# Fifteen conditioning chunks as VectorE multiply-and-sum steps, and context tiles in the router's waits

## The reference, cut to what matters

```python
def ada_params(cond, w, b):             # cond 1024, w 1024 x 6144, b 6144
    m = jax.nn.silu(cond) @ w + b
    return jnp.split(m, 6, axis=-1)     # shift1, scale1, gate1, shift2, scale2, gate2

h = modulate(rms_norm(x, g), sh1, sc1)          # h * (1 + sc1) + sh1
p = h @ w_in + b_in                             # first block: 1024 -> 6656
...
h2 = modulate(rms_norm(x, g2), sh2, sc2)
x = x + gt2 * moe_ffn(h2)               # 32 experts in 4 groups, two per token
```

## Time and profile before

| | |
|---|---|
| Three runs | 1829.98, 1832.39, 1832.53 us; median 1832.39 |
| The profiled execution | span 1829.5 us from the first to the last instruction; a device time of its own is not given, so the shortest run, 0.5 us above the span, stands for it |
| TensorE busy | 1767.4 us, 97% of the span |
| VectorE busy | 462.7 us, 25% |
| ScalarE busy | 324.7 us, 18% |
| HBM read | 470.29 MB; 257 GB/s over the span |
| Mean granted TensorE clock | 0.996 of full speed |

### The profile page before, as it was taken

The page is one execution under the profiler, slowest core; times in us unless marked ns, Lnnn a source line. Parts: engine busy times, 40 slices in busy tenths (PEclk is TensorE's granted clock), DMA queues, the critical chain, the costliest instruction groups (busy, mean ns, idle before and its releaser), DMA issues. The chain is left out here.

```text
span 1829.5 us, 24606 instructions
## 1 busy us (share of the span) xinstructions
PE 1767.4 (97%) x10866; PEld 1344.7 (73%) x10866; DVE 462.7 (25%) x1010; ACT 324.7 (18%) x732; POOL 0.2 (0%) x4
## 2 busy tenths in 40 slices
PE   6999999999999999999999999999999999999997
PEld 4674887888664466676667577688888876888886
DVE  5310124525125221111101144531100135411001
ACT  4110013103214111010000123521100125211000
POOL 0000000000000000000000000000000000000000
PEclk9999999999999999999999999999999999999999
DMA  9453677467999999999999973365444331554430
GB/s 380 177 224 116 259 316 280 185 253 268 372 391 414 401 421 420 421 421 421 398 421 407 421 291 118 139 241 181 153 161 140 113 116 46 215 200 161 142 111 23
DMA packets 61810, 472.93 MB, mean 259 GB/s; under 512 B 7719, under 2 KB 11208, under 8 KB 12040
## 3 DMA queue, kind: packets, MB, share of 16 engines
q1 hardware_dynamic: 60472, 470.08, 65.7%
q10 hardware_dynamic: 1232, 1.28, 0.2%
HBM read 470.29 MB, written 1.05 MB: 258 GB/s over the span
## 5 line engine op out<-in xcount | busy, mean ns | idle before, releaser
L2520 PE MATMUL bank<-hT,ring 128*128 128x256 f32 x1024 | 221.5, 379 | 0.0
L2539 PE MATMUL bank<-second_work,ring 128*128 128x256 f32 x1024 | 221.3, 379 | 0.0
L2539 PEld LDWEIGHTS bank<-second_work,ring 128*128 128x128 f32 x1024 | 194.6, 190 | 26.5
L2520 PEld LDWEIGHTS bank<-hT,ring 128*128 128x128 f32 x1024 | 194.4, 190 | 26.4
L1345 PE MATMUL bank<-hT,ring 128*128 128x256 f32 x704 | 160.8, 385 | 4.5 <-issue 2.7
L1345 PEld LDWEIGHTS bank<-hT,ring 128*128 128x128 f32 x704 | 133.1, 192 | 39.8 <-issue 12.9
L650 PE MATMUL bank<-hT,ring 128*128 128x256 f32 x704 | 153.9, 379 | 0.0
L650 PEld LDWEIGHTS bank<-hT,ring 128*128 128x128 f32 x704 | 133.5, 191 | 18.8 <-issue 1.2
L1813 PE MATMUL bank<-ring,rowsT 128*32 128x512 f32 x1008 | 117.5, 597 | 1.2 <-DMA ring<-in_expert_w 1.0
L1345 PE MATMUL bank<-tmp,ring 128*128 128x256 f32 x384 | 86.5, 382 | 5.9 <-DMA ring<-in_w_out 4.3
L1345 PEld LDWEIGHTS bank<-tmp,ring 128*128 128x128 f32 x384 | 71.9, 190 | 24.8 <-DMA ring<-in_w_out 7.8
(11 more groups left out here) (468 smaller groups left out, 1707.5 us busy)
## 6 DMA issues: line engine op xcount, KB each, us to landing
ring<-in_expert_w SPq DMA_DIRECT2D x190, 1024.0 KB, 12.2
ring<-in_w_ff SPq DMA_DIRECT2D x96, 1024.0 KB, 7.1
ring<-in_ada_w SPq DMA_DIRECT2D x36, 2048.0 KB, 10.4
ring<-in_w_in SPq DMA_DIRECT2D x29, 1024.0 KB, 8.2
ring<-in_w_in SPq DMA_DIRECT2D x13, 2048.0 KB, 8.8
ring<-in_w_out SPq DMA_DIRECT2D x12, 1024.0 KB, 6.0
ring<-in_ret_w_o SPq DMA_DIRECT2D x2, 2048.0 KB, 8.2
ring<-in_w_out SPq DMA_DIRECT2D x2, 2048.0 KB, 12.8
```

The costliest lines, as they stand in the source:

```text
L2520: mm = pe.matmul(ff_bank(n), w[:, k, (n % 2) * P:(n % 2 + 1) * P], hT[:, k, xs], start=k == 0, stop=k == DT - 1)
L2539: mm = pe.matmul(ff_bank(FT + i), w[:, f, :], W[:, 16 * h + f, :], start=h == f == 0, stop=h == 1 and f == FT // 2 - 1)
```

## The change

The 12 chunks A0 to A11 and the three of the router stage are no longer multiplied on TensorE. The host stores their 15 weights transposed (`rows_first`), so that a 2 MB chunk R holds 4 x 128 output features, one per partition, with the 1024 inputs along it. The condition vectors (three of them) are loaded as rows that stand in all partitions, and ScalarE applies Silu to them. VectorE then does, for each 128 features and each condition needed, one `scalar_tensor_tensor` over 1024 columns with a sum (`accum_out`) into `mods`. R0 to R6 belong to `ada_w_2` and need both conditions, 8 steps each; R7 to R14 belong to `ada_w` and need one, 4 steps each: 88 steps.

All 15 stand in the input stage now. The order of the ring there is W0 W1 R0 W2 R1 W3 R2 R3 W4 R4 R5 W5 R6 W6 R7 W7 R8 R9 W8 R10 W9 R11 R12 W10 R13 R14 W11 W12. The steps of an R chunk are dealt evenly over the tiles of the W chunk that follows it: VectorE does them behind the emptying of each tile. An R chunk's slots are free when its last step is done. In the router stage TensorE does (-1, 0) first, (-1, 1) and (-1, 2) behind the token transposes, (-1, 3) behind the ranks and (0, 0) behind `gather(0)`.

```diff
+        ROW_CHUNKS = [(1, j) for j in range(4)] + [(0, j) for j in range(3)] + [(None, j) for j in range(8)]
...
         plan_both("in", [wide("w_in", j) for j in IN_CHUNKS],
-                  [wide("ada_w", j) for j in range(ADA0, 12)] + [wide("ada_w_2", j, 1) for j in range(4)],
-                  [0, 0, 1, 1, 1, 1, 1, 1, 2, 1, 1, 1, 1])
+                  [features_first(("ada_wT_2_0", "ada_wT_2_1", "ada_wT")[-1 if l is None else l], j) for l, j in ROW_CHUNKS],
+                  [0, 1, 1, 2, 2, 1, 1, 2, 1, 2, 2, 0, 0])
...
-        plan_both("ada2_router", [wide("ada_w_2", j, 0) for j in range(8, 12)], in2_views[0][0:2], [0, 0, 0, 2])
+        plan_both("ada2_router", [wide("ada_w_2", 8, 0)], in2_views[0][0:2], [2])
...
+                    row_steps = [(n, i, m) for n, job in enumerate(row_jobs) for i in range(4) for m in range(len(job[3]))]
...
+                        follows = min(t[0] for t in tiles if t[0] > job[0])
+                        tiles_of_next[n] = [i for i, t in enumerate(tiles) if t[0] == follows]
...
+                    def row_steps_after(i):
+                        here = [s for s, (n, _, _) in enumerate(row_steps) if i in tiles_of_next[n]]
+                        if not here:
+                            return range(0)
+                        where = tiles_of_next[row_steps[here[0]][0]]
+                        done = lambda t: here[0] + len(here) * t // len(where)
+                        return range(done(where.index(i)), done(where.index(i) + 1))
+
+                    def weigh(dve, s):
+                        n, i, m = row_steps[s]
+                        chunk, mod, first, conds = row_jobs[n]
+                        if i == m == 0:
+                            wait_chunk(dve, chunk)
+                        w = chunk_tile(chunk, D)[:, i, :]
+                        if len(conds) == 2 and s >= 2:
+                            dve.wait_ge(S("weighed"), s - 1)
+                        nc.vector.scalar_tensor_tensor(out=w if m == len(conds) - 1 else products_out, in0=w, scalar=1.0,
+                                                       in1=cond_rows[conds[m]], op0=ALU.mult, op1=ALU.mult,
+                                                       accum_out=mod[:, first + i, m:m + 1]).then_inc(S("weighed"), 1)
...
+                        for s, (n, i, m) in enumerate(row_steps):
+                            freed[row_jobs[n][0]] = (S("weighed"), s + 1)
...
-                                for n in due(i):
-                                    if n == 0:
-                                        pe.wait_ge(S("hy_spec_out"), 4)
-                                    beside.pe(pe, n)
... (SyncE, ahead of the early tables and of W1)
+                            for m in (0, 2, 3):
+                                sp.dma_start(cond_rows[m], a["cond_rows"][m:m + 1, :].to_broadcast([P, D]))\
+                                    .then_inc(S("rows_loaded"), 16)
... (VectorE's loop over the tiles)
-                                for n in due(i):
-                                    beside.dve(dve, n)
+                                if i == N_KEYS + TT:
+                                    dve.wait_ge(S("cond_rows"), 3)
+                                for s in row_steps_after(i):
+                                    weigh(dve, s)
... (ScalarE: waits ahead of the tiles of W12; Silu behind the keys)
+                                    if i == len(tiles) - 4:
+                                        act.wait_ge(S("weighed"), len(row_steps))
...
+                                if i == N_KEYS + 1:
+                                    act.wait_ge(S("rows_loaded"), 64)
+                                    for m in (0, 2, 3):
+                                        nc.scalar.activation(cond_rows[m], cond_rows[m], ACT.Silu).then_inc(S("cond_rows"), 1)
... (router stage, TensorE)
-                        ada.pe(pe, 0)
-                        ada.pe(pe, 1)
-                        ada.pe(pe, 2, turns=False)
-                        ada.turn(pe, 1)
+                        ctx_pe(pe, -1, 0)
...
-                        ada.turn(pe, 2)
-                        ctx_pe(pe, -1, 0)
-                        pe.wait_ge(S("logits_read"), TT)
                         ctx_pe(pe, -1, 1)
+                        ctx_pe(pe, -1, 2)
...
-                        ctx_pe(pe, -1, 2)
+                        ctx_pe(pe, -1, 3)
...
-                        ctx_pe(pe, -1, 3)
+                        ctx_pe(pe, 0, 0)
```

More of the change, by code:

```diff
@@ L554, in build @@
                                  for i in range(4)]
[L556 to L559, removed]
+                    row_of = lambda x: x.rearrange("p a t -> p (a t)")
@@ new lines, in build @@
+                    cond_rows = {0: row_of(tmp[:, 6:8, :]), 2: row_of(gates[:, 12:16, :]), 3: row_of(tmp[:, 0:2, :])}
+                    products_out = row_of(tmp[:, 2:4, :])
+                    row_jobs = [(c, mods[0], 4 * (ADA0 + j), (0,)) if l is None else (c, (mods[1], mods[2])[l], (36, 0)[l] + 4 * j, (2, 3))
+                                for c, (l, j) in zip(at["in_beside"], ROW_CHUNKS)]
+                    row_steps = [(n, i, m) for n, job in enumerate(row_jobs) for i in range(4) for m in range(len(job[3]))]
@@ L560, in build @@
                     order = [e for e, _ in evac]
                     nb = 4
[L563 to L568, removed]
+                    tiles_of_next = {}
+                    for n, job in enumerate(row_jobs):
+                        follows = min(t[0] for t in tiles if t[0] > job[0])
+                        tiles_of_next[n] = [i for i, t in enumerate(tiles) if t[0] == follows]
@@ L893, in _ @@
                                     nc.scalar.activation(Dm[:, :, :], Dm[:, :, :], ACT.Exp)
-                                for n in due(i):
-                                    beside.act(act, n)
+                                if i == N_KEYS + 1:
+                                    act.wait_ge(S("rows_loaded"), 64)
+                                    for m in (0, 2, 3):
+                                        nc.scalar.activation(cond_rows[m], cond_rows[m], ACT.Silu).then_inc(S("cond_rows"), 1)
                             act.wait_ge(S("router_b_loaded"), 16)
@@ L1474, in ctx_act @@
                         ins.then_inc(K("evac_s"), 1)
-                    if g == 0 and i == 1:
+                    if g == 0 and i == 3:
                         act.wait_ge(K("lam_sums"), 1)
@@ L1508, in ctx_dve @@
                     nc.vector.tensor_reduce(lam_sum[:, :], lam_tmp[:, :, :], AX_X, ALU.add).then_inc(K("lam_sums"), 1)
-                elif g == 0 and i == 2:
+                elif g == 1 and i == 0:
                     dve.wait_ge(K("lam_exp"), 1)
@@ L2022, in _ @@
                                 .then_inc(S("tok_out"), 1)
+                        ctx_act(act, -1, 0)
                         act.wait_ge(S("group_shifted"), 1)
                         do(nc.scalar.activation(wide4[2], wide4[0], ACT.Exp), "group_exp")
+                        ctx_act(act, -1, 1)
                         act.wait_ge(S("top_gap"), 1)
                         do(nc.scalar.activation(small[:, :, 6:7], small[:, :, 5:6], ACT.Exp), "gap_exp")
-                        for n in range(3):
-                            ctx_act(act, -1, n)
+                        ctx_act(act, -1, 2)
+                        ctx_act(act, -1, 3)
                         for n in range(QUADS // 2):
@@ L2049, in _ @@
                         rows(0)
-                        ctx_act(act, -1, 3)
                         for q in range(QUADS + 1):
@@ L2967, in tiles, with rows_first @@
     return w.reshape(*w.shape[:-2], w.shape[-2] * n)
+def rows_first(w):
+    return w.T.reshape(-1, 4, P, D).transpose(0, 2, 1, 3).reshape(-1, P, 4 * D)
 def up_pieces(w):
@@ L3008 @@
         "router_rows": np.concatenate([x["router_expert_b"], x["router_group_b"]], 1).reshape(1, -1),
+        "cond_rows": np.concatenate([x[n].reshape(1, D) for n in ("c", "c_ctx", "c_2", "c_ctx_2")], 0),
+        "ada_wT": rows_first(x["ada_w"][0][:, 2 * D:]), "ada_wT_2_0": rows_first(x["ada_w_2"][0][:, 9 * NCOLS:]),
+        "ada_wT_2_1": rows_first(x["ada_w_2"][1][:, 0:2 * D]),
         "base": base, "const1": const1, "early": early, "const2": const2, "feats": feats,
@@ L3014 @@
         "rpb": rpb, "sgu_b": sgu_b, "sgu_wT": x["sgu_w_2"].transpose(3, 0, 1, 2),
[L3015 removed]
+        "ada_w": tiles(x["ada_w"][0][:, 0:2 * D], NCOLS), "w_in": tiles(x["w_in"][0], NCOLS), "ret_w_o": tiles(x["ret_w_o"][0], NCOLS),
         "hy_w_o": tiles(x["hy_w_o"][0], D), "w_out": tiles(x["w_out"][0], NCOLS),
```

35 lines of the change are left out of this document (14 added, 21 removed).

## The result

The changed kernel takes 1852.2 us (median of 4 runs, 1850.2 to 1859.6), the kernel before 1832.5 (median of 4, 1830.0 to 1832.7): ratio 1.0119, 95% interval 1.0101 to 1.0137. The change makes it slower by 1.2%; the forecast was 1855.

A forecast was written before the change was run, and what follows sets the result against it. TensorE was taken to bound the input stage, with DMA and TensorE both near their limits in the experts' part. Terms -25.1 + 46.0 + 8 - 6.6 = +22.3 took the span from 1829.5 to 1851.8, median 1855, range 1838 to 1878.

The forecast's parts named there:

- The removed products, -25.1: Input stage: eleven chunks at 2.05 us off TensorE, about 22.5, plus 2.6 at the stage's end.
- The price of a step, 1.30 us: VectorE, input stage: each multiply with sum over 1024 columns takes 1.30 us, range 1.2 to 2.4.
- the second rival: Input stage: the sum halves VectorE's rate, 2.4 us a step, 116 us late, total 1925; 8 in 100.
- Late weights, 46.0 us: Input stage: ring slots come free late, so TensorE waits for W chunks, 46.0 us in sum, longest 14.1 at W5.
- my walk: Input stage: chunk-by-chunk reckoning of slot release, issue and landing, with 1.30 us steps and 8.0 us landings; sum 46.0 late.
- The clock, +8: Input stage: TensorE loses about 2 us behind each long pause; four pauses count, +8 us, ends 0 and 14.
- The router, -6.6: Router stage: logits 3.1 us earlier and a context tile of 3.5 us moved into a wait; ends -4 and -8.
- the sign I named for it: Router stage: the first expert product would stand 35.2 - 6.6 = 28.6 us behind the stage's start.
- Relief of the loads, 0: Experts' part: three chunks fewer, 6.3 MB or 15 us of DMA, counted at nothing; bounds 0 to -10.
- The first rival: Input stage: VectorE frees R chunks early enough, nothing is late, removed products win, -31.7, total 1801; 8 in 100.

The follow-up runs named there:

- e6_no_row_loads: Changed kernel without the R chunks' loads, steps multiplying columns of xT instead; total 5258.0 us, not comparable; input stretch 180.24 us against 206.43 before the change.
- e4_router_old: Changed kernel with the router part undone: its three conditioning chunks loaded and multiplied on TensorE again, context tiles in their old places; 1861.8 us, ratio 1.0171 to before.
- e3_both: Changed kernel with another order of loads and up to 8 steps behind each of the first tiles of the next W chunk; 1814.3 us, ratio 0.9888 to before.
- e8_steps_doubled: e3_both with each VectorE step issued twice, the second waiting for the first; 1897.3 us, ratio 1.0337 to the kernel before.
- e10_half_filled: Changed kernel with 14, 28, 8, 20, 7 and 4 useless TensorE products ahead of the waits for W4, W5, W7, W8, W9, W10; 1870.4 us.
- e11_both_filled: e3_both with 7 and 9 useless TensorE products ahead of the waits for W10 and W12; 1814.3 us, ratio 0.9897 to the kernel before.
- e1_front: Changed kernel, same load order, with up to 8 steps behind each first tile of the next W chunk instead of dealt evenly; 1836.6 us, ratio 1.0016 to before.

## Why the prediction was right

The mechanism and the sign held, and the size came out close, in part by luck: 1852.2 against 1855, the span 1848.4 against 1851.8, with errors in the terms that went opposite ways.

- *The removed products, -25.1.* Measured 26.2 in e6_no_row_loads. A chunk cost more than 2.05 us: before the change tiles of neighbouring W chunks started 15.96 us apart, and without it 13.82.
- *The price of a step, 1.30 us.* Mis-sized. It is 1.145 us from start to start: 1.22 like the `tensor_tensor` of the earlier trace rows, with 0.08 of overlap, and the reading of the sum (0.08) lies beside the next step. The low end of my range, 1.2, was already above it. The Trainium skill, Vector Engine (DVE) Microarchitecture Reference, § Points that are easy to get wrong, would have halved the rate: for this form, 128x1024 f32 with a sum, the trace does not bear it out, and the second rival falls with it.
- *Late weights, 46.0 us.* 38.99. Chunk by chunk, forecast and seen: W4 7.9 and 6.5, W5 14.1 and 13.0, W7 4.9 and 3.9, W8 10.0 and 9.2, W9 4.3 and 3.5, W10 2.9 and 2.2, W11 1.2 and 0.7. All seven are a little high, by the price of the step and by the landing: W5, W8 and W9 had their first product 7.5 to 7.7 us behind the issue, not 8.0. At W4 two errors met: the steps freed its slots 2.8 us earlier than in my walk, and the load took 1.5 us longer. The two smallest terms (W1 0.4, W6 0.3) show as no pause. The fixed part of 2.0 us in the Trainium skill, DMA: Bandwidth & Descriptors, § Anatomy of one DMA — SWDGE (gpsimd) path, was measured there on transfers issued by GpSimd, and these are issued by SyncE. With it a load would take an estimated 5.0 + 2.0 = 7.0, which is 0.5 to 0.7 us under what the trace shows.
- *The clock, +8.* Mis-sized: 11.2 by the lengths of the groups, of which what W9's tiles lost fell into the next wait. I had counted four pauses with an effect; the trace shows six chunks with longer tiles, W4 to W10 but for W6. The least pause with one was 2.19 us, W10's.
- *The router, -6.6.* 6.9. Its parts are right too: 3.1 ahead of the gather, and 3.85 from the first expert product on, where the moved tile's 3.5 was expected. But the sign I named for it was wrong: I put the first expert product 28.6 us behind the stage's start, taking both parts off, though the moved tile still stands ahead of that product. It stands at 32.05, which is 35.15 - 3.1.
- *Relief of the loads, 0.* TensorE's waits for loads in the experts' part are 13.3 us against 12.4 before, and e4_router_old shows no relief by the chunks' absence.
- *The first rival* ("decides at W5: late unless R3 is used up by 144") was false for this kernel, and it is nearly what e3_both does. I gave it 8 in 100 for a mistake of mine; as a kernel it exists, two edits away.

Against the forecast span the removed products took 1.1 us more, the late weights were 7.0 less, the router gave 0.3 more, and the other way the clock cost 3.2 more and some 1.8 lie outside the terms (1.3 of counting, as under e6_no_row_loads, and 0.6 by which W2 starts later): 3.4 us below. The late weights and the clock are the two terms that were mis-sized, and that they offset each other is luck.

## What to carry to other kernels

Where loads go round a ring of a few slots, moving the use of a chunk to an idle engine moves the return of its slot too: ask for each chunk when its last use ends, who stands so many places behind it, and whether that load lands before its own use. An engine's idle time says little of this; with VectorE busy for 135 of 236 us TensorE was held up for 39. Where such a change loses, as here, first place the new steps as early as their data allow and reorder the ring, before giving it up.

## What the hardware showed that I had not expected

- The granted clock falls inside a pause and stays down behind it. In the changed kernel, stretch by stretch as in the earlier trace rows:

```profile
155.00:160.00 5.00, 0.00 (x0) 0.00 (x0) 5.00 (x8) 0.00 (x0) 0.00 (x0) 0.72 0.00 0
160.00:164.00 4.00, 0.00 (x0) 0.00 (x0) 0.19 (x2) 0.00 (x0) 0.00 (x0) 0.50 0.75 246
168.00:172.00 4.00, 4.00 (x6) 1.78 (x7) 0.00 (x0) 0.00 (x0) 0.00 (x0) 0.64 0.88 377
```

  0.50 is the lower level, 1.2 GHz. In the input stages the pauses of 2.19 us and more cost 1.5 to 3 us behind them, with two exceptions (3.37 us in e4_router_old and 2.23 in e8_steps_doubled, 0.1 or less lost); those of 2.12 us and less cost 0.1 at most.
- The length of a pause does not decide it alone. In the experts' part every kernel has the same pause of 1.78 or 1.79 us, where a product waits for ScalarE. Behind it the clock stayed at 1.00 for the next 12 us in four profiled executions (before, after, e10_half_filled, e11_both_filled). In eight others it fell to 0.50 for 3 to 7 us, and in e1_front for 19. First the changed kernel, then e1_front; TensorE's busy time is the second column of the stretches:

```profile
591.51 0.63 PE L1642 MATMUL bank<-base,ctx_work 128*128 128x128 f32 x4 [1.79 <-ACT ctx_work L1687]
591.50:600.00 8.50, 8.37 (x62) 3.02 (x62) 4.71 (x15) 4.83 (x19) 0.00 (x0) 1.00 1.02 421
576.33 0.63 PE L1642 MATMUL bank<-base,ctx_work 128*128 128x128 f32 x4 [1.78 <-ACT ctx_work L1687]
578.00:597.00 19.00, 19.00 (x80) 6.02 (x76) 8.14 (x24) 5.88 (x23) 0.00 (x0) 0.50 1.01 414
```

  From the mixing stage's start to the end e1_front's profiled execution took 1536.2 us and the changed kernel's 1526.6. Among e1_front's ten executions the span goes from 1828.6 us at a mean clock of 0.990 to 1842.8 at 0.982, while span times clock stays within 1807 to 1814. So the spread between executions of one kernel, up to 0.8% here, goes in large part with the clock. Why it falls behind this pause in one execution and not in another stays open.
- One f32 product appears as two records in the trace. A price per product has to be taken from the length of a group and the count of products in the code, not from the count of records.
